# A hybrid mixer in front of a mixture of experts: new order of the input slabs, one slab moved from the inverse into the chunk waits

## The reference, cut to what matters

```python
proj = h @ w_in                                   # (512, 1024) x (1024, 2952)
xa, ga, q, k, v, fl, pc = split(proj)             # 256, 256, 512, 512, 512, 8, 896 columns
# LRU: conv of 4 taps, two sigmoid gates, a scan, gated by gelu(ga)
xc = conv(xa); r = sigmoid(xc @ wa + ba); i = sigmoid(xc @ wx + bx)
a = exp(-8 r softplus(-lam)); b = sqrt(-expm1(2 log a)) * i * xc; y = gelu(ga) * scan(a, b)
# attention: q, k normed per head, bias c = cumsum(logsigmoid(fl)), 8 heads of 64, causal
# RWKV-7: p += (prev - p) * mu; r, k, v and three low-rank inputs wd, ad, gd from pc
w = decay(tanh(wd) @ w2); a = sigmoid(a0 + ad @ a2); g = sigmoid(gd) @ g2
state = state * w + (state @ -kk) b^T + v k^T     # per token; chunks of 64 in the kernel
```

## Time and profile before

| | us |
|---|---|
| median of three runs (lowest, highest) | 2724.15 (2721.8, 2726.65) |
| the profiled execution | 2731.68 |
| its span, first to last instruction | 2729.8 |
| PE busy in it | 2656.8 (97%) |
| DVE, ACT, POOL busy | 1530.0, 1087.6, 899.1 |
| mean granted PE clock | 0.979 |

### The profile page before, as it was taken

One profiled execution on the slowest core, in us unless ns is written; L12 is line 12 of the kernel. 1 busy time (PEld: TensorE's weight loads), 2 busy tenths in 40 slices (PEclk: granted clock), 3 DMA queues, 4 the chain that ended last, 5 costly groups with the idle time before them and its releaser, 6 DMA issues.

```text
span 2729.8 us, 34577 instructions
## 1 busy us (share of the span) xinstructions
PE 2656.8 (97%) x14006; PEld 2215.2 (81%) x14006; DVE 1530.0 (56%) x1692; ACT 1087.6 (40%) x1271; POOL 899.1 (33%) x205
## 2 busy tenths in 40 slices
PE   7799989999999999999999999999999999999998
PEld 6686778888788988888888888898988888888887
DVE  3775554899882374355473355744483354645445
ACT  3433353788633442334342222425432343422222
POOL 2221011000033244344444444332444444444444
PEclk9899788999999999999999999999999999999998
DMA  4231013899421364223233333221562332233332
GB/s 149 85 125 40 1 69 124 314 369 369 180 78 73 116 240 169 92 92 118 95 113 126 128 115 116 104 93 53 203 253 77 106 113 97 108 116 116 123 130 101
DMA packets 61299, 361.27 MB, mean 132 GB/s; under 512 B 7280, under 2 KB 8176, under 8 KB 26096
## 3 DMA queue, kind: packets, MB, share of 16 engines
q1 hardware_dynamic: 58720, 353.51, 35.3%
q10 hardware_dynamic: 2448, 5.90, 0.6%
HBM read 357.27 MB, written 2.10 MB: 132 GB/s over the span
## 4 chain that ended last, share of the span: by engine, by line
PE 79%; DVE 4%; ACT 1%; issue 1%; ACTq 0%; DVEq 0%
PE pd L270 19%; PE pd L271 19%; PE pd L272 19%; PE pd L291 2%; PE pd L290 2%; PE pd L289 2%; PE pd L2125 2%; PE pd L2124 2%; PE pd L2123 2%; DVE sb_y_lo L1855 2%; DVE sb_h_lo L543 1%; PE pd L2150 1%; PE pd L2152 1%; PE pd L2151 1%; PE pd L2080 1%
## 5 line engine op out<-in xcount | busy, mean ns | idle before, releaser
L224 POOL TENSOR_TENSOR sb_w_lo<-sb_raw,sb_w_hi 128x2048 fp32r<-128x2048 f32 x184 | 860.1, 4675 | 1733.3 <-ACT sb_w_hi L215 1733.3
L270 PE MATMUL pd<-sb_h_hi,sb_w_hi 128*128 128x512 f32 x1600 | 634.5, 397 | 9.1 <-DVE sb_h_lo L543 5.1
L272 PE MATMUL pd<-sb_h_hi,sb_w_lo 128*128 128x512 f32 x1600 | 624.7, 390 | 0.0
L271 PE MATMUL pd<-sb_h_lo,sb_w_hi 128*128 128x512 f32 x1600 | 624.6, 390 | 0.0
L215 ACT CAST sb_w_hi<-sb_raw 128x2048 fp32r<-128x2048 f32 x185 | 353.5, 1911 | 351.5 <-PE pd L272 325.9
L270 PE MATMUL pd<-sb_y_hi,sb_w_hi 128*128 128x512 f32 x960 | 376.7, 392 | 8.0 <-DVE sb_y_lo L1866 3.9
L271 PE MATMUL pd<-sb_y_lo,sb_w_hi 128*128 128x512 f32 x960 | 374.6, 390 | 0.0
L272 PE MATMUL pd<-sb_y_hi,sb_w_lo 128*128 128x512 f32 x960 | 374.6, 390 | 0.0
L270 PEld LDWEIGHTS pd<-sb_h_hi,sb_w_hi 128*128 128x128 f32 x1600 | 301.6, 188 | 77.7 <-issue 6.6
L272 PEld LDWEIGHTS pd<-sb_h_hi,sb_w_lo 128*128 128x128 f32 x1600 | 301.3, 188 | 63.5
L271 PEld LDWEIGHTS pd<-sb_h_lo,sb_w_hi 128*128 128x128 f32 x1600 | 301.7, 189 | 62.6 <-issue 1.9
(11 more groups left out here) (575 smaller groups left out, 3881.4 us busy)
## 6 DMA issues: line engine op xcount, KB each, us to landing
sb_raw<-in_slabs SPq DMA_DIRECT2D x190, 1024.0 KB, 4.8
sb_moe_raw<-in_moe SPq DMA_DIRECT2D x56, 1024.0 KB, 5.0
sb_raw<-in_moe SPq DMA_DIRECT2D x28, 1024.0 KB, 4.9
sb_QK<-in_ada SPq DMA_DIRECT2D x32, 512.0 KB, 5.3
sb_V<-in_ada SPq DMA_DIRECT2D x32, 512.0 KB, 5.5
sb_M<-in_ada SPq DMA_DIRECT2D x16, 512.0 KB, 3.3
sb_Y<-in_ada SPq DMA_DIRECT2D x16, 512.0 KB, 5.5
sb_MG<-in_ada SPq DMA_DIRECT2D x16, 512.0 KB, 5.6
```

The source lines that it names most:

```text
L224: pool.tensor_tensor(w_lo[j][:], raw[j][:], w_hi[j][:].bitcast(F32), ALU.subtract).then_inc(w_lo_ready[j], 1)
L270: pe.matmul(out, w_hi[j][:, cols], hi[:, k], start=(k == 0), stop=False)
L271: pe.matmul(out, w_hi[j][:, cols], lo[:, k], start=False, stop=False)
L272: last = pe.matmul(out, w_lo[j][:, cols], hi[:, k], start=False, stop=(k == KT - 1))
```

## The change

- **Slabs in another order**: (0, 0) misc, (0, 1) k, (1, 0) r, (1, 1) v, then k and v for attention as before, (4, 0) and (4, 1) q, (5, 0) the LRU input, (5, 1) the LRU gate branch.
- **Opening**: PE runs only (0, 0) alone; the low-rank products stand in (0, 1), the kk sums behind six pieces of (1, 0), the bonus sums in (2, 0), and the transposes of v in (2, 1), ahead of `scaled`. ACT stores and splits one slab at a time (`split` of (m + 1, j) behind the store of (m, j)). DVE shifts tiles as they arrive: 6; 2 and 3; 0 and 1; 4 and 5. The decay constant goes into the scale of ACT's exponentials; DVE's multiply by it is gone.
- **Inverse**: 24 pieces instead of 32, mostly one a step. ACT stores and splits after n = 7 and n = 14, not 5, 10 and 15. The convolution (DVE) and the gelu (ACT) are no longer in it; eight squares are in steps 17 to 19, behind the last `ada_begin`.
- **Chunks**: the eight pieces of slab (5, 1) stand in chunks 0 to 2, the convolution among DVE's chunk copies, and chunk 3 with the gates and spreads ahead of attention (`BESIDE = 4`). The gates use two banks in turn. ACT makes both decays and both gelus behind the last copy of q and k, so just ahead of the first exponential of attention.
- **Buffers**: q goes straight to `T[:, 0:4]`; POOL's move of q is gone, its zero fill is two halves. `lb_one`, `lb_over`, `lb_product` and `lb_root` move one unit later.

The core of the diff:

```diff
-        BESIDE = 3
+        BESIDE = 4
...
-            def fill(n, first, count):
-
-                m, j = 4 + n // 10, n // 5 % 2
-                for k in range(first, first + count):
+            def late_pieces(first, count):
+
+                for p in range(first, first + count):
+                    m, j, k = 4 + p // 16, p // 8 % 2, p % 8
...
+            def filled(n):
+                return 24 * n // (TB * INVERSE_LEVELS)
...
+                late_pieces(filled(n), filled(n + 1) - filled(n))
...
             chunk_s(0)
+            late_pieces(24, 2)
             chunk_w(1)
             chunk_o(0)
+            late_pieces(26, 1)
             chunk_u(1)
             chunk_known(1)
+            late_pieces(27, 1)
             chunk_s(1)
+            late_pieces(28, 2)
+            chunk_w(2)
+            chunk_o(1)
+            late_pieces(30, 1)
+            chunk_u(2)
+            chunk_known(2)
+            late_pieces(31, 1)
+            chunk_s(2)
             qk_spreads(0)
             qk_spreads(1)
+            chunk_w(3)
+            chunk_o(2)
             qk_spreads(2)
+            lru_gate(0)
+            chunk_u(3)
+            chunk_known(3)
             qk_spreads(3)
+            lru_gate(1)
+            chunk_s(3)
...
-                if n == 5:
-                    act.wait_ge(negc_ready, 1)
-                    store_late(4, 0, lru_x)
-                    split_next(act, 4, 1)
-                if n == 10:
-                    store_late(4, 1, lru_g)
-                    split_next(act, 5, 0)
-                if n == 15:
-                    store_late(5, 0, q_tmp)
...
+                if n == 7:
+                    store_late(4, 0, q_raw[:, 0:2])
+                    split(act, 5, 0)
+                if n == 14:
+                    store_late(4, 1, q_raw[:, 2:4])
+                    split(act, 5, 1)
...
             chunk_out(0)
-            gate(2)
-            gate(3)
-            decay(0)
             chunk_out(1)
+            store_late(5, 1, lru_g)
             per_head(0)
             per_head(1)
+            chunk_out(2)
+            for n in range(4):
+                per_head(2 + n)
+                gate(n)
+            per_head(6)
+            per_head(7)
+            decay(0)
             decay(1)
-            for p in range(2, 8):
-                per_head(p)
+            act.wait_ge(slab_out[1], IN1_PAIRS)
+            for j in range(2):
+                act.activation(gelu[:, j], lru_g[:, j], ACT.Gelu_apprx_tanh).then_inc(lru_gelu, 1)
```

More of the change, by code:

```diff
@@ L791, in _ @@
             last.then_inc(lora_g, 1)
-            pieces(2, 0, 6, 2)
+            pieces(0, 1, 6, 2)
+            pieces(1, 0, 0, 6)
             pe.wait_ge(gate_a, 2)
@@ L802, in _, with turn_tokens @@
                 pe.matmul(px[j][:], blk[:], bonus[:, j], start=True, stop=True).then_inc(bonus_sum, 1)
-            pieces(2, 1, 4, 4)
+            pieces(2, 0, 4, 4)
+            def turn_tokens(n, src):
+                j = n % 2
+                if n >= 4:
+                    pe.wait_ge(tr_out, n - 3)
+                for b in range(TB):
+                    last = pe.transpose(px[(n + 2) % 4][:, b * P:(b + 1) * P], src[:, j, b * P:(b + 1) * P], ident[:])
+                last.then_inc(tr_done, 1)
+            pieces(2, 1, 0, 5)
+            pe.wait_ge(kk_root, 2)
+            pe.wait_ge(shifted, 7)
+            for n in range(2):
+                turn_tokens(n, A[:, 4:6])
+            pieces(2, 1, 5, 3)
             slab_starts(pe, 3, 0)
@@ L807, in _ @@
             pe.wait_ge(scaled, 2)
[L808 to L817, removed]
+            for n in range(2, 6):
+                turn_tokens(n, k_s if n < 4 else b_s)
             token_piece(pe, 0, 1, h_hi, h_lo)
@@ L1149, in store @@
                 last.then_inc(slab_out[j], 1)
[L1151 to L1167, removed]
+            split(act, 0, 1)
+            act.wait_ge(c_row_first_loaded, 16)
+            act.activation(c_row_first, c_row_first, ACT.Silu).then_inc(c_row_first_ready, 1)
+            act.wait_ge(slab_done[0], 1)
+            act.copy(A[:, 6], pd[0][:])
+            act.wait_ge(fl_in, 1)
+            act.activation(fl[0:8], pd[1][0:8], ACT.Identity,
+                           bias=v1("fox_fb", rows=slice(0, 8))).then_inc(slab_out[0], 1)
+            split(act, 1, 0)
+            act.wait_ge(shifted, 1)
             act.activation(T[0:32, 3], A[0:32, 6], ACT.Tanh)
             act.copy(T[32:64, 3], A[32:64, 6]).then_inc(lora_in, 1)
-            act.activation(T[64:128, 3], A[64:128, 6], ACT.Sigmoid)
-            split_next(act, 2, 0)
+            act.activation(T[64:128, 3], A[64:128, 6], ACT.Sigmoid).then_inc(lora_gate_in, 1)
             act.wait_ge(lora_w, 1)
@@ L1177, in _ @@
                 act.activation(B_a[:, j], px[2 + j][:], ACT.Sigmoid, bias=v1("a0", j)).then_inc(gate_a, 1)
+            store(0, 1, A[:, 2:4])
+            split(act, 1, 1)
             act.wait_ge(lora_g, 1)
@@ L1184, in _, with keep_tokens @@
             for j in range(2):
+                act.wait_ge(cum_ready, j + 1)
+                act.activation(QR[:, j, 1], cum[:, j], ACT.Exp, scale=LOG_DECAY)
+                act.activation(k_s[:, j], cum[:, j], ACT.Exp, scale=-LOG_DECAY)
+                act.activation(d_end[:, j], cum[:, j, CH - 1::CH], ACT.Exp, scale=LOG_DECAY)
+                act.wait_ge(prev_ready, j + 1)
+                act.activation(QR[:, j, 0], b_s[:, j], ACT.Exp, scale=LOG_DECAY).then_inc(decays, 1)
+            store(1, 0, A[:, 0:2])
+            split(act, 2, 0)
+            for j in range(2):
                 act.wait_ge(kk_sum, j + 1)
                 act.activation(T[:, j], px[2 + j][:], ACT.Sqrt).then_inc(kk_root, 1)
-            store(2, 0, k_att[:, 0:2])
[L1188 to L1195, removed]
-            store(2, 1, k_att[:, 2:4])
[L1197 to L1201, removed]
+            store(1, 1, A[:, 4:6])
+            split(act, 2, 1)
+            def keep_tokens(n, dst):
+                act.wait_ge(tr_done, n + 1)
+                act.mul(dst[:, :, (n % 2) * P:(n % 2 + 1) * P], px[(n + 2) % 4][:].rearrange(
+                    "p (a b) -> p a b", a=TB), -1.0 if n >= 4 else 1.0).then_inc(tr_out, 1)
+            store(2, 0, k_att[:, 0:2])
+            split(act, 3, 0)
+            for n in range(2):
+                keep_tokens(n, v_tok)
+            store(2, 1, k_att[:, 2:4])
+            split(act, 3, 1)
+            for n in range(2, 6):
+                keep_tokens(n, k_tok if n < 4 else b_tok)
             def store_tokens(m, j):
@@ L1433, in _ @@
                 v(dve.tensor_tensor(b_s[:, j], cum[:, j], B_dec[:, j], ALU.subtract), prev_ready, j + 1)
+            dve.wait_ge(slab_out[1], 1)
+            shift((2, 3), 2)
+            for j in range(2):
+                v(dve.tensor_scalar(kk[:, j], A[:, 2 + j], v1("kk", j), None, ALU.mult), kk_raw, j + 1)
             dve.wait_ge(gate_a, 2)
@@ L1437, in _ @@
                 v(dve.tensor_tensor(A[:, 2 + j], A[:, 2 + j], T[:, 2], ALU.mult))
+            dve.wait_ge(slab_out[0], 2)
+            shift((0, 1), 4)
+            for j in range(2):
                 v(dve.scalar_tensor_tensor(bonus[:, j], A[:, j], v1("rk", j), A[:, 2 + j], ALU.mult, ALU.mult),
```

179 lines of the change are left out of this document (84 added, 95 removed).

## The result

The changed kernel takes 2736.52 us (median of 14 runs), the kernel before 2725.2 in the runs beside it: ratio 1.004, with an interval of 1.0027 to 1.0053. It is 11 us slower. (One of the 14 runs of the kernel before took 6299.24 us; it doesn't move the median.) The forecast was 2721.5, with a range of 2711 to 2731, and most of the chance on same (0.45) and faster (0.35): the time is outside the range and on the other side.

What follows compares the result with a forecast made beforehand. The prediction took TensorE, busy 97% of the span, as the bound, so only its idle time and half clock could move. Terms -13.5 + 14.0 - 5.4 + 2.1 = -2.8 against median 2724.15 gave 2721.5 us, range 2711 to 2731.

Steps and rivals of the forecast that it cites:

- Opening, -13.5: Before the Gram matrices: 15.2 us idle and 2.1 of half clock removed, 3.8 of new waits; -17.3 to -7.7.
- Inverse, +14.0: Steps 14 and 15: rows queued behind a later slab load idle TensorE 9.0 us, plus half clock; +6 to +26.
- second rival: Inverse, step 14: rows arrive in time, so neither the wait nor its half clock comes; 2710.2 us, chance 0.12.
- Chunks 0 to 2, -5.4: Chunks ahead of attention: dense pieces end the half-clock stretch from 262.50, convolution costs nothing; 0 to -5.4 us.
- price of half clock, 0.43: Anywhere on TensorE: share of busy time wasted at half clock, from product starts 0.97 and 1.71 us apart.
- Attention, +2.1: Start of attention: old half-clock stretches go (-5.6, -5.8), new ones cost 8.7 and idle 4.8 us; -11 to +12.
- ScalarE starving attention: Start of attention: late gates expose ScalarE's tail, TensorE idles 7 us, three half-clock stretches; 2732.3 us, chance 0.18.
- the clock stays up: Spreads and chunks: no low stretch until attention is under way, so 8.7 us isn't paid; about 2713 us, chance 0.20.
- the opening that gives half: Opening: both new waits at 4.79 us and another at `scaled`, -7.4 instead of -13.5; 2727.5 us, chance 0.05.

Runs made afterwards that it cites:

- ada_first: Changed kernel with SP's load of the rows for steps 14 and 15 issued ahead of the waiting slab load: 2727.87 us, ratio 1.0004.
- spread_rows: Changed kernel with the eight spreads (norm-scale products) over 128 rows, the added ones zeros, instead of 16: 2724.21 us, ratio 0.9992.
- rows64: Changed kernel with the eight spreads over 64 rows, the added ones zeros, instead of 16: 2722.42 us, ratio 0.9986.
- beside3: Changed kernel with chunk 3 put back beside the first unit of attention, pieces, gates and spreads left as changed: 2738.8 us, ratio 1.0033.

## Why the prediction was wrong

- **Opening, -13.5: right** (-13.7). Two waits went, two smaller ones came (1.67 + 2.33 = 4.0 where I put 3.8), and nothing is late at `scaled`. From 42 us on, TensorE's idle time fell by 11.5 us and its busy time by 2.2.
- **Inverse, +14.0: right** (+12.8), and for the reason given: the rows behind the slab in SP's queue. The stall is 7.77, not 9.0, since the row was there 1 us sooner than the value I took between its bounds. The whole stage has 9.3 more idle (forecast 11.0) and 3.5 of half clock (forecast 3.0). But only some 2 of these 3.5 lie behind the stall; the others come from a low stretch at 145 to 149, near the start of the inverse, that the forecast didn't have. That this part came out so near is luck. ada_first takes the stall away alone. So the second rival (rows in time) is refuted, and with it the gain of the change as it stands.
- **Chunks 0 to 2, -5.4: the step that failed.** Its words were "The half-clock stretch from 262.50 came among small products; with dense pieces in their place I let it go". The pieces weren't put in the place of the small products but ahead of them: the spreads, the gates and now chunk 3 stand together behind the last piece. What brings the low clock there is the spreads' 16 rows (spread_rows and rows64 take it away), and these the change doesn't touch. That part of the stage takes 28.56 us, and 16.38 in spread_rows. The row that could have told was in view: the fall at 262, 5 us after the first product marked 16*128, with TensorE at 24.19 of 24.40 busy. I noted that no gap explained it and then asked about density and not about what had just begun. With the spreads on 128 rows the term is 6.4 - (28.56 - 16.38) = -5.8: the figure was that of a kernel without the cause.
- **The price of half clock, 0.43, was too small.** It compared starts in unlike places: the 0.97 is from a spread that comes behind a product of another kind, the 1.71 is in the midst of a row of spreads, where two starts are only 0.86 apart at full clock (272.31 and 273.17 in spread_rows). Like with like, a spread behind the chunk's products and the gate behind it, TensorE in order of time, first in spread_rows at full clock, then in the changed kernel at half:

```profile
263.06 1.12 PE L933 MATMUL px<-sb_M,sb_W 128*128 128x512 f32 x2
264.02 1.02 PE L923 MATMUL pd<-sb_Y,sb_c 128*128 128x512 f32 x2
```
```profile
261.76 2.07 PE L928 MATMUL px<-sb_M,sb_W 16*128 16x512 f32 x2
263.76 2.08 PE L918 MATMUL pd<-sb_Y,sb_c 128*128 128x512 f32 x2
```

  The starts are 0.96 and 2.00 apart, so the share is 0.52 (0.50 by 0.86 and 1.71). Of the 23.90 us busy in the low window that is 12.4, and 12.2 were measured.
- **Attention, +2.1: near** (+3.3), by two errors that cancel. The idle at `chunk_known(4)` was 2.04, not 4.8; the low stretches were 23.65 and 7.50 long, not one and a half of 13.5. In all, the stage has 1.8 more idle, where 4.8 was forecast, and 1.5 more busy time beyond chunk 3, where the forecast had 2.7 less. At full clock the wait is 5.60 (spread_rows), so 4.8 was near for a TensorE that arrives on time.
- **The rivals.** The slower one, ScalarE starving attention, named the right side and a time of 2732.3, but not the cause: it wanted a wait over 5 us, and there were 2.04. That the clock stays up was right only for spreads on 64 rows or more. A case was missing: the small products keep their low clock, and chunk 3, put among them, pays it too (by beside3 it would have paid as much at the low start of attention). One sum among the rivals is wrong besides: for the opening that gives half, both waits at 4.79 and one more of 3.14 make -17.3 + 9.6 + 3.1 = -4.6 and not -7.4, so its time was 2730.3 and not 2727.5. Nothing of this rival came.
- **The range.** Its lower half rested on the clock, its upper half on a wait. The term of the chunks had the bounds 0 and -5.4, with no loss on the other side, though a longer low stretch was as open as none. It cost 12.2, and that is why the time lay outside.

Not tried by itself: the new opening without the rest. That it gives 13.7 us rests on the stage marks of the traces.

## What to carry to other kernels

When a stretch at the lower clock starts with no idle time ahead of it, look at which products began just before it, by the rows and columns they use, and not only at how dense the work is. Work that is packed in behind such products pays the low clock too; here zeros up to 64 or 128 rows cost TensorE nothing and took it away in the changed kernel. When a step moves, read every queue's list for what stands behind the load that now waits: two lines swapped in SP's list were worth 8.7 us.

## What the runs showed of the hardware

Products on 16 rows, with products on 64 and 128 rows between them, were followed by a fall of TensorE's clock from 2.4 to 1.2 GHz, 2 to 5 us after the first of them and with no idle time ahead of it, in five traces of four kernels (that before, the changed one twice, ada_first, beside3). With 64 and 128 rows the clock stayed at 2.4 GHz through the same 14 to 16 us, in seven traces of six kernels. Few rows aren't the only thing that goes with a fall under load: at 313.00 to 326.50 before and 319.00 to 326.50 after, the clock is low with TensorE wholly busy and no product on 16 rows near. What brings it down there isn't shown, and neither is by what measure 16 rows do. The Trainium skill (TensorE: Matmul & The Clock Gate, "Why this matters for your kernels") tells of idle gaps as what brings the clock down. The trace agrees at 210.00 to 217.00, in the wait of 7.77, and differs at 261.00, where there was none.
